# Products of a constant tile in the linear-attention stage of a two-layer step on one Trainium2 core

## The reference, cut to what is computed

```python
def step(s, chunk):
    qc, kc, vc, lac = chunk
    bc = jnp.cumsum(lac, axis=2)
    o_inter = jnp.einsum('bhtk,bhkv->bhtv', qc * jnp.exp(bc), s)
    decay = jnp.exp(jnp.where(mask, bc[:, :, :, None, :] - bc[:, :, None, :, :], -jnp.inf))
    a = jnp.einsum('bhtk,bhsk,bhtsk->bhts', qc, kc, decay)
    o = o_inter + jnp.einsum('bhts,bhsv->bhtv', a, vc)
    b_end = bc[:, :, -1]
    s_new = jnp.exp(b_end)[..., None] * s + jnp.einsum('bhsk,bhsv->bhkv', kc * jnp.exp(b_end[:, :, None, :] - bc), vc)
    return s_new, o
```

## Time and profile before

| | |
|---|---|
| median of 3 runs | 1422.97 us (1421.21 to 1423.62) |
| the profiled execution, its own time | 1421.89 us |
| its span, first to last instruction | 1420.3 us |
| mean granted TensorE clock over the span | 0.984 |
| PE busy | 1371.3 us (97%) |
| DVE, ACT, POOL busy | 848.0 us (60%), 527.8 us (37%), 110.6 us (8%) |
| the GLA stage, about 234 to 299 us of the span | 65 us |

### The profile page before, as it was taken

How to read it: one execution, slowest core, us unless ns; L and a number is a source line. 1 busy time by engine, 2 the same in 40 slices (tenths; PEclk the granted TensorE clock), 3 DMA queues, 4 the chain that set the end, 5 groups by cost and what they waited for, 6 DMA issues and landing times.

```text
span 1420.3 us, 28954 instructions
## 1 busy us (share of the span) xinstructions
PE 1371.3 (97%) x11466; PEld 1314.0 (93%) x11466; DVE 848.0 (60%) x1284; ACT 527.8 (37%) x860; POOL 110.6 (8%) x158
## 2 busy tenths in 40 slices
PE   7999999989999999999999999997999999999997
PEld 7899998889999999999998778875999999999997
DVE  7565558856666666432364888887456666664221
ACT  5434445534332223322234565563432233222110
POOL 0221113111000000000001010000200000000000
PEclk9999998999999999999999999997999999999999
DMA  6566544122222223322127778772222222233320
GB/s 223 129 143 136 102 170 106 63 73 87 95 89 89 90 98 108 107 81 96 60 93 221 243 225 277 239 214 83 93 87 95 97 89 89 89 107 112 117 76 22
DMA packets 47369, 170.86 MB, mean 120 GB/s; under 512 B 6382, under 2 KB 7710, under 8 KB 47306
## 3 DMA queue, kind: packets, MB, share of 16 engines
q1 hardware_dynamic: 38938, 143.61, 29.7%
q0 software_dynamic: 8368, 26.38, 9.2%
HBM read 158.45 MB, written 11.51 MB: 120 GB/s over the span
## 4 chain that ended last, share of the span: by engine, by line
PE 88%; DVE 5%; issue 2%; ACT 2%; DMA 1%; POOL 0%; SPq 0%; DVEq 0%; ACTq 0%; POOLq 0%
PE ps L539 57%; PE ps L590 16%; PE ps L722 2%; PE ps L947 1%; PE ps L962 1%; PE ps L977 1%; PE ps L911 1%; PE ps L950 1%; PE ps L956 1%; DMA qb<-q_rows 1%; PE ps L1080 1%; DVE w_lo L1697 1%; ACT w_hi L1193 1%; DVE s_prod L2262 1%; PE ps L684 0%
## 5 line engine op out<-in xcount | busy, mean ns | idle before, releaser
L1697 DVE TENSOR_TENSOR w_lo<-raw,w_hi 128x1024 fp32r<-128x1024 f32 (+1 forms) x189 | 244.4, 1293 | 351.3 <-ACT w_hi L1193 351.3
L539 PE MATMUL ps<-h_hi,w_hi 128*128 128x260 f32 x1536 | 434.6, 283 | 0.8 <-DVE h_lo L1730 0.7
L539 PE MATMUL ps<-h_hi,w_lo 128*128 128x260 f32 x1536 | 434.0, 283 | 0.0
L539 PE MATMUL ps<-h_lo,w_hi 128*128 128x260 f32 x1536 | 432.4, 282 | 0.0
L1193 ACT CAST w_hi<-raw 128x1024 fp32r<-128x1024 f32 (+1 forms) x189 | 208.2, 1101 | 229.5 <-PE ps L539 223.3
L539 PEld LDWEIGHTS ps<-h_hi,w_hi 128*128 128x128 f32 x1536 | 289.0, 188 | 1.8 <-DVE h_lo L1730 1.1
L539 PEld LDWEIGHTS ps<-h_hi,w_lo 128*128 128x128 f32 x1536 | 288.8, 188 | 0.0
L539 PEld LDWEIGHTS ps<-h_lo,w_hi 128*128 128x128 f32 x1536 | 288.8, 188 | 0.1
L539 PE MATMUL ps<-a_lo,w_hi 128*128 128x260 f32 x704 | 199.0, 283 | 0.0
L539 PE MATMUL ps<-a_hi,w_hi 128*128 128x260 f32 x704 | 198.7, 282 | 0.0
L539 PE MATMUL ps<-a_hi,w_lo 128*128 128x260 f32 x704 | 198.7, 282 | 0.0
(11 more groups left out here) (399 smaller groups left out, 2178.5 us busy)
## 6 DMA issues: line engine op xcount, KB each, us to landing
raw<-in_w_ffn SPq DMA_DIRECT2D x88, 512.0 KB, 3.6
raw<-in_w_down SPq DMA_DIRECT2D x32, 704.0 KB, 4.1
k_pages<-in_cache_k SPq DMA_DIRECT2D x32, 512.0 KB, 5.4
v_pages<-in_cache_v SPq DMA_DIRECT2D x32, 512.0 KB, 7.2
raw<-in_w_rec_in SPq DMA_DIRECT2D x29, 512.0 KB, 6.5
raw<-in_w_att_kv SPq DMA_DIRECT2D x24, 512.0 KB, 5.4
raw<-in_w_rec_out SPq DMA_DIRECT2D x8, 512.0 KB, 3.7
raw<-in_w_att_q SPq DMA_DIRECT2D x8, 512.0 KB, 3.7
```

The source lines that it names most:

```text
L539: ins = TE.matmul(half(bank, h), w_part[:, buf, w], m_part[:, k_at + k, h * HALF:(h + 1) * HALF], start=start, stop=stop)
L1697: V.tensor_tensor(w_lo[:, n % 2, 0:nk * P], raw[:, n % RAW, 0:nk * P], w_hi[:, n % 2, 0:nk * P].bitcast(F32), ALU.subtract).then_inc(lo_sp ...
```

## The change

A helper `keep_busy(n, bank, at)` issues `n` float32 products of the constant tile ONES (128x128) with the identity (128 columns) into 128 columns of a PSUM bank. Their result is overwritten or not read. They use all 128 rows and columns of the array. It is called in three places, and the loops of `sample_outputs` change places, so that the samples' products go alternately to the two row halves.

```diff
+            def keep_busy(n, bank, at=3):
+
+                for _ in range(n):
+                    TE.matmul(ps[:, bank, at * P:(at + 1) * P], ONES, IDENT, start=True, stop=True)
...
                 near_levels(p, (2, 3), 3)
+                if p == 0:
+                    keep_busy(16, 5)
                 near_levels(p, (4, 5), 5)
 
                 wait(pe, dD, "qk_far", p)
                 wait(pe, rD, "m5" if p else "m0")
                 for c in range(NC_G):
+                    keep_busy(2, 0)
                     for hh in range(2):
...
                 wait(pe, gD, "n0", p)
                 wait(pe, gD, "ss", p)
-                for hh in range(2):
-                    r = slice(64 * hh, 64 * hh + 64)
-                    for b in range(B):
+                for b in range(B):
+                    if b == B // 2:
+                        keep_busy(4, 5, 0)
+                    for hh in range(2):
+                        r = slice(64 * hh, 64 * hh + 64)
                         ins = TE.matmul(ps[:, 5 + hh, 384 + b:385 + b], g_ss[r, b, :], z[r, 16 + p, T + b:T + b + 1],
                                         start=True, stop=True)
```

## The result

The changed kernel takes 1425.03 us, median of 20 executions (1420.14 to 1431.97). The kernel before, executed 20 times by then, has a median of 1420.38 (1418.21 to 1423.62), lower than the 1422.97 of the three that stood at the start. The ratio is 1.0027, 95% interval 1.0017 to 1.0037: slower by a quarter of a per cent, where 0.17% faster was forecast. 1425.03 lies outside the range.

A forecast was written before the change was run, and what follows sets the result against it. PE, 88% of the chain, was taken as the bound, slowed by 1.2 GHz stretches. Gains of 0.2 + 0.4 + 1.8 = 2.4 us against the median of 1422.97 gave 1420.6 us, 8-in-10 range 1418.3 to 1423.7.

The forecast's parts named there:

- sixteen products: Between near A and near B of pair 0: 32 records at 0.117 us each plus 0.18 for shape changes, 3.93 us.
- near A's start to near B's end: Pair 0's near levels with the sixteen products between them: from 234.14 to 239.99 us, nearly no cost against before.
- a far group: Two products ahead of each far chunk, both pairs: 0.65 us, of which 0.18 for changes of shape.
- far levels with groups, pair 0, pair 1: Far levels of both pairs: 3.44 us at full clock, 6.04 us with four groups.
- samples with four products: Samples' stage of each pair, alternating row halves plus four products: 2.95 us instead of 3.32, 0.4 gained per pair.
- clock behind pair 0's samples: After pair 0's samples the clock stays full, so `early(4)` takes 3.08 us instead of 4.36, 1.3 us gained.
- clock behind pair 1's samples: After pair 1's samples the clock stays full in L750 and `early(7)`, 1.8 us gained.
- `early(6)`: Pair 1, behind near C: starts at 279.6 instead of 279.81 us, added groups eating all but 0.2 us of the gain.
- the stop itself: PE idle 2.9 us inside pair 0's near levels, taken for late instruction supply; it was to hide the sixteen products' 3.93 us.
- the stop stays and the clock falls: Rival, 8%: near B of pair 0 stops 3.5 us behind the sixteen products, far levels run at slow clock; 1429.5 us.
- The clock falls after the samples: Rival, 24%: clock drops behind the samples despite the four products; 1423.5 us if both drops stay, 1422 to 1422.5 if one.
- Free changes of shape: Rival, 24%: weight loads hide behind running products, so the 0.18 us vanishes and far stages shorten by 0.7 each; 1418.8 us.

The follow-up runs named there:

- e5: The changed kernel without the two products ahead of each far chunk of pair 1; 1426.12 us, ratio 1.0016 to the kernel before.
- e11: The changed kernel without the products ahead of the far chunks of either pair; 1424.12 us, ratio 1.0 to the kernel before.
- e1: The changed kernel with no added products, only the samples' products alternating between row halves; 1419.01 us, ratio 0.9975 to the kernel before.
- e7: e1 with 136 more semaphore instructions that wait for nothing, ahead of GLA in PE's program; 1425.51 us, ratio 1.002 to the kernel before.
- e8: e7 with DVE draining bank 0 ahead of the slab's split and the far factors; 1421.48 us, ratio 0.9984 to the kernel before.
- e9: The changed kernel timed again on another chip, with a second profile; 1427.41 us, ratio 1.0022 to the kernel before.
- e6: e1 with the last third of early(1), eight needed products, moved between pair 0's near A and near B; 1418.85 us, ratio 0.9964 to the kernel before.
- e12: e6 with DVE draining bank 0 ahead of the slab's split and the far factors; 1418.67 us, ratio 0.9964 to the kernel before.
- e3: The kernel before plus only the sixteen products between near A and near B of pair 0; 1425.04 us, ratio 1.0021 to the kernel before.
- e4: The kernel before plus only two products ahead of each far chunk, both pairs; 1429.45 us, ratio 1.0047 to the kernel before.
- e10: The changed kernel with eight products instead of sixteen between near A and near B; 1428.01 us, ratio 1.0032 to the kernel before.
- e2: e1 with the four products in the middle of the samples kept; 1421.43 us, ratio 0.999 to the kernel before.

## Why the prediction was wrong

Terms of the sum, against the profile after (with its later start of 0.36 us taken off):

| term | forecast | measured |
|---|---|---|
| sixteen products | 3.93 us | 3.77 |
| near A's start to near B's end | 5.85 | 7.88 |
| a far group | 0.65 | 0.64 (242.38 to 243.02) |
| far levels with groups, pair 0, pair 1 | 6.04 | 6.06, 6.03 |
| samples with four products | 2.95 | 3.06 |
| clock behind pair 0's samples | full | full |
| clock behind pair 1's samples | full | 0.50, L755 3.18 us |
| `early(6)` | 279.6 | 281.3 |

**The step that failed** is the one on the sixteen: "Cost against before: nearly nothing ... The cover is the stop itself". In the good execution near B ended 2.0 us later than forecast, and in the profiles of e5 and e11 by another 1.4 and 2.3 us (9.3 and 10.2 us behind near A's start), with the clock lost. The products ran beside the stop in part only; PE still stopped behind them, with no semaphore to wait for. The rule that I had drawn from one trace, a stop at a fixed instruction that ends at a fixed time, was wrong on both counts: across the profiles here it stands in near B, in the far levels or in near C, and lasts from 0.2 to 4.2 us.

In the profile after, two terms make up the miss: 2.4 us less were forecast, 1.5 more came, and of the 3.9 between them 2.0 are near B and 1.9 the clock behind pair 1's samples, where L755 and `early(7)` take 6.6 us (293.60 to 300.18, the wait of 0.79 taken off) and not 4.6. The median is 2 us above this execution; what the longer executions add, no profile of the changed kernel shows.

The Trainium skill, "Runtime: NRT & Kernel Launch", section "Instruction fetch mechanics", says that an engine's program streams in blocks of 256 instructions, and that the cost of crossing into one is mostly hidden. If the supply is the cause, the near and far levels, at 0.015 us a record in the near ones, are where it was not hidden here: all fourteen profiles have idle time without a releaser in pair 0's `within`. The traces tie it to the fetch in this much. Most stops end soon behind the fetch of a block: 0.2 us (before), 1.3 to 1.4 (e1, both of e7, e8, e9), 1.8 and 1.9 (e5, e11). And the fetch near 238 us itself is a slow one. An execution has 44 or 45 fetches of such blocks, with a median of 1.0 us; this one took 1.6 us in the profile after, 4.0 in e5 and 5.0 in e11, the two with stops of 3.15 and 3.20 us, and in nine of the fourteen profiles it is the longest of all. A packet's time is its share times 16 engines times the window, here 1.8 us (237.6 to 239.4, after) and 4.1 us (239.7 to 243.8, e5):

```profile
q8 instruction: 1, 0.02, 5.6%
q8 instruction: 1, 0.02, 6.1%
```

It is no rule: e6 has a fetch of 4.2 us and a stop of 0.59, and in e12 the stop of 1.7 us has no fetch in it, from 239.3 us on. What holds the instructions back is open.

**A wait that the stop had hidden** was missing from the prediction. It took pair 0's far levels as ready when near B ended. The drain m0 comes 4.0 us after near A's start (e1), so the stop of 3.5 us never cost 3.5; without it PE would have waited for DVE. In the kernel before this drain ended at 237.96, and the far levels began at 240.13:

```profile
237.27 0.69 DVE L2068 TENSOR_TENSOR x<-x,ps 128x520 f32<-128x520 f32 x1
```

So 2.2 us and the clock were all that was to be gained there, and sixteen products with near A and near B need 5.9 us even when nothing stops, 1.9 more than DVE leaves room for. e3 shows the balance: the sixteen alone are 0.21% slower.

**Pair 1** went as worked out in the profile after: the groups ran at full clock and 2.6 us of work came on PE. But the price was set against a lucky profile. Of the ten kernels here without groups in pair 1, only the kernel before has its near C at full clock in the profile (1.16 us for 64 records; 1.65 to 1.99 in the others, e1 to e3, e5 to e8, e11 and e12), and they need 11.6 to 13.5 us from near A to `chunk_states` where it needed 11.07. With the groups the clock held in after and e9 (12.93 us) and not in e4 and e10 (14.3). e11 against e9 puts both pairs' groups at 3.3 us, between the worked-out work of 5.2 and the clock that they hold.

**The samples**: the alternation was sized rightly (0.062 against 0.058 a record) but its worth was not. By itself it is 3.7 us (e1), 2.8 of it in the length of the two stages in the profile; with four products in the middle it is 1.2 (e2). I had charged the four products 1.1 us a pair and paid them back with 3.1 us of clock. They do hold the clock: behind the samples it is full in 11 of 12 places in the profiles of the six kernels that have them (after, e2, e5, e9, e10, e11), the one fall being that of pair 1 in after. What was wrong is the worth of it. A fall costs 1.2 to 1.5 us in `early(4)` and some 1.6 in L755 and `early(7)`, and with the alternation alone (e1, e6, e7, e8, e12) it came in 6 of 10 places. My estimate from these is 0.9 us saved a pair for 1.1 spent.

**The rivals**: "the stop stays and the clock falls" had 8% and comes nearest to what e5 and e11 show. It was priced at 1429.5 us (its terms add up to 1429.7), where e5's and e11's profiled executions took 1430.3 and 1427.0. The error was to treat it as a case that holds or doesn't: by the clocks of the executions something like it may hold in about half of them, with the median between the two; no profile of such an execution of the changed kernel was taken. "The clock falls after the samples" (24%) held in one place of two in the profile. "Free changes of shape" is refuted by the 0.64 us a group.

The forecast was also set against a median of three executions, 1422.97, where twenty had 1420.38. Set against twenty, the same forecast would have been 2.6 us lower and the miss larger: the change was forecast at 2.4 us less and measured at 3.8 us more (0.27% of 1420), or 4.65 by the two medians.

## What to carry to other kernels

Products that only keep the clock up are work of PE, and they pay only where they run inside a wait that is there in every execution, which one trace cannot show; look at the engine behind the stop (here DVE's drain) for how long the place really is. Work that is needed anyway can stand there at no cost, as in e6 and e12. A clock that one profile shows at a place is not yet what the kernel does there: look at a second profile before a price rests on it. The part of this change that paid was the order of the row halves, alone.

## What the runs showed of the hardware that was not expected

- Idle time on PE with no semaphore behind it, 0.2 to 4.2 us at a time, nearly all in pair 0's `within` (e7 and e8 have 0.2 us elsewhere), and placed differently from profile to profile. With 136 instructions put in far ahead of it the kernel takes some 6 us of 1420 more (e7 against e1, by ratios), how much of it by the stops is open.
- The fetch of a 16 KB block of instructions takes 1.0 us as a rule (median of 45 in the profile after), and up to 5.0 at this one place (e2, e11).
- The executions of one kernel differ by 5 to 12 us on one chip, along with a mean granted clock between 0.978 and 0.991.
- A record of a 64x128 float32 product with one column takes 0.104 us when its neighbours use the same row half and 0.062 in turn with the other.
- A group of two full products between half-row ones costs 0.64 us at 2.4 GHz and 1.15 at 1.2.
